# A decoder step on one core: the u projection in whole 128-column blocks, and the Toeplitz rows moved in their queues

## The reference, cut to what matters

```python
z = jnp.einsum('ntd,de->nte', h, w_in)       # columns: q | k | v | u
att = dilated_attn_prompt(q, k, v, rel_bias)  # scores + bias, softmax, values, per head
ssm_y, hT_re, hT_im = s5_branch(u, h0, ...)   # scan over positions, four steps fused by the kernel
x = x + g1 * jnp.einsum('nte,ed->ntd', mixed, w_out)
```

## Time and profile before

| | |
|---|---|
| Time, 3 runs | 965.74, 966.4 (median), 970.36 us |
| Profiled execution | 969.46 us, of which the span from first to last instruction is 967.6 us |
| Mean granted TensorE clock | 0.872 of full speed |
| Busy | PE 789.9 us (82%), DVE 278.7, POOL 166.9, ACT 153.2 |
| Chain that ended last | PE 74%, DVE 8%, DMA 6%, POOL 5% |

### The profile page before, as it was taken

How to read it: one execution, slowest core, us unless ns; L and a number is a source line. 1 busy time by engine, 2 the same in 40 slices (tenths; PEclk the granted TensorE clock), 3 DMA queues, 4 the chain that set the end, 5 groups by cost and what they waited for, 6 DMA issues and landing times.

```text
span 967.6 us, 11960 instructions
## 1 busy us (share of the span) xinstructions
PE 789.9 (82%) x4890; PEld 467.8 (48%) x4890; DVE 278.7 (29%) x693; ACT 153.2 (16%) x324; POOL 166.9 (17%) x258
## 2 busy tenths in 40 slices
PE   2499999999689679676689994499999999999900
PEld 2295688888355355555434554343443444344300
DVE  3633223200012222575313635411111111111028
ACT  1321000000022233313221210000101010000123
POOL 1324100000593000165600000100000000000053
PEclk9878999999655979788899975599999999999955
DMA  9950376700920621709152239667698999999552
GB/s 324 380 181 29 137 223 236 266 4 2 378 107 12 254 83 37 300 3 377 30 162 88 94 126 341 251 238 270 236 397 306 402 401 395 402 399 395 215 196 92
DMA packets 83134, 212.17 MB, mean 219 GB/s; under 512 B 3516, under 2 KB 9948, under 8 KB 80997
## 3 DMA queue, kind: packets, MB, share of 16 engines
q1 hardware_dynamic: 70118, 181.46, 50.9%
q0 software_dynamic: 5472, 19.16, 5.7%
q10 hardware_dynamic: 7488, 10.77, 3.0%
HBM read 197.18 MB, written 17.86 MB: 222 GB/s over the span
## 4 chain that ended last, share of the span: by engine, by line
PE 74%; DVE 8%; DMA 6%; POOL 5%; issue 3%; SPq 3%; ACT 2%; ACTq 0%; POOLq 0%; DVEq 0%
PE ps L2285 17%; PE ps L2288 11%; PE ps L1941 6%; PE ps L1933 6%; PE ps L2195 5%; PE ps L1813 5%; DMA toeplitz<-g_d 3%; PE ps L1902 3%; PE ps L1974 3%; PE ps L1972 3%; PE ps L1992 2%; PE ps L1826 2%; SPq L531 2%; DMA ring<-in_w_out 1%; PE ps L2035 1%
## 5 line engine op out<-in xcount | busy, mean ns | idle before, releaser
L2285 PE MATMUL ps<-ering,xgT 128*128 128x512 f32 x256 | 115.1, 605 | 2.5 <-ACT xgT L801 1.7
L2285 PEld LDWEIGHTS ps<-ering,xgT 128*128 128x128 f32 x256 | 48.6, 194 | 63.4 <-issue 60.1
L2288 PE MATMUL ps<-ering,xgT 128*64 128x512 f32 x320 | 70.7, 595 | 1.2 <-ACT xgT L801 1.2
L1941 PE MATMUL ps<-hT,ring 128*32 128x136 f32 x1024 | 63.1, 424 | 0.0
L1933 PE MATMUL ps<-hT,ring 128*128 128x272 f32 x256 | 59.2, 393 | 0.0
L1941 PEld LDWEIGHTS ps<-hT,ring 128*32 128x32 f32 x1024 | 52.1, 128 | 10.5
L2285 PE MATMUL ps<-ering,aT 128*128 128x512 f32 x128 | 56.2, 593 | 0.0
L768 POOL DMA_INDIRECT xg<-h_d,gidx x13 | 12.3, 949 | 242.8 <-PE ps L1813 210.0
L1933 PEld LDWEIGHTS ps<-hT,ring 128*128 128x128 f32 x256 | 48.5, 190 | 10.3 <-issue 0.4
L1974 PE MATMUL ps<-toeplitz,const 128*128 128x128 f32 (+3 forms) x64 | 32.5, 598 | 25.2 <-DMA toeplitz<-g_d 25.2
L1826 PE MATMUL ps<-ring,silu_c 128*32 128x128 f32 x768 | 27.8, 310 | 24.7 <-DMA ring<-in_ada_w 24.7
(11 more groups left out here) (436 smaller groups left out, 1161.0 us busy)
## 6 DMA issues: line engine op xcount, KB each, us to landing
ering<-in_w_gate SPq DMA_DIRECT2D x16, 2048.0 KB, 17.4
ering<-in_w_up SPq DMA_DIRECT2D x16, 2048.0 KB, 17.4
ering<-in_w_down SPq DMA_DIRECT2D x16, 2048.0 KB, 20.8
ring<-in_ada_w SPq DMA_DIRECT2D x12, 2048.0 KB, 13.1
ring<-in_cache_k SPq DMA_DIRECT2D x8, 1792.0 KB, 10.5
ring<-in_cache_v SPq DMA_DIRECT2D x8, 1792.0 KB, 11.5
ring<-in_w_in SPq DMA_DIRECT2D x4, 2048.0 KB, 22.3
y_d<-ysb ACTq DMA_DIRECT2D x26, 256.0 KB, 6.1
```

The lines of the kernel that those rows point to most:

```text
L1941: ins = mm(out[32 * j:32 * j + 32, N4 * i:N4 * (i + 1)], r[:, c0:c0 + 32], hT[:, k, j::TDEC], start=k == 0, stop=k == KD - 1, tile_positio ...
L2285: return mm(out, lhsT=lhs, rhs=ering[slots[0]][:, cols], start=k == 0, stop=k == n - 1)
L2288: ins = mm(out[c, :], lhsT=lhs[:, c], rhs=ering[slot][:, cols], start=k == 0, stop=k == n - 1, tile_position=(0, HT_ * half))
```

## The change

1. **u in whole blocks.** u is computed as q and k are: 128 by 128 stationary blocks against 272 consecutive tokens. The step interleave is made in the eviction: for each of the four channel groups r of a block and each step j, one copy reads 32 partitions by 68 columns of PSUM with a stride of four columns and writes them to partitions 32 j of u4. So ACT and DVE have 16 copies each for a block, where they had one each.
2. **Toeplitz rows.** SP issues those of heads 0 and 1 before slab 2. Those of heads 2 to 7 leave SP: ACT issues head h's after its last instruction of step 4 (h - 2) + 3. SP then has the slabs alone.

```diff
+    def by_step(z, c, r, j, half):
+        n = HALF // TDEC
+        return (u4[32 * j:32 * j + 32, 4 * c + r, n * half:n * (half + 1)],
+                ps[32 * r:32 * r + 32, 6 * half + z % 2, j:HALF:TDEC])
...
-        for i in (IT_KV + 2, IT_KV + 3):
-            item(i)
-        for h in range(HEADS):
-            if h >= 2:
-                sp.wait_ge(s("S"), QT * (h - 1))
-            sp.dma_start(toep[:, h % 2, :], ...).then_inc(s_toep[h % 2], 16)
-            if h == 3:
-                for i in range(IT_KV + 4, IT_KV + 8):
-                    item(i)
-        for i in range(IT_KV + 8, IT_WO):
+        for h in range(2):
+            sp.dma_start(toep[:, h, :], ...).then_inc(s_toep[h], 16)
+        for i in range(IT_KV + 2, IT_WO):
             item(i)
...
+                for r in range(4):                       # ACT, and DVE with half 1
+                    for j in range(TDEC):
+                        dst, src = by_step(z, c, r, j, 0)
+                        ins = f(dst, src, ACT.Copy)
+                ins.then_inc(s("za"), 1)
...
             f(PTs[:, st % 2, 0:m], ps[:, 2 + st % 2, 0:m], ACT.Copy).then_inc(s("ptr"), 1)
+            if st % QT == QT - 1 and st < QT * (HEADS - 2):
+                h = st // QT + 2
+                act.wait_ge(s("S"), QT * (h - 1))
+                act.dma_start(toep[:, h % 2, :], ...).then_inc(s_toep[h % 2], 16)
...
-                    for k in range(KD if kind != U_ else 0):
+                    for k in range(KD):
                         ins = mm(out, r[:, 512 * k + P * c:512 * k + P * (c + 1)], hT[:, k, cols],
                                  start=k == 0, stop=k == KD - 1)
-                    for i in range(2 if kind == U_ else 0):
-                        for k in range(KD):
-                            c0 = 512 * k + P * c + 32 * (2 * n + i)
-                            for j in range(TDEC):
-                                ins = mm(out[32 * j:32 * j + 32, N4 * i:N4 * (i + 1)], r[:, c0:c0 + 32],
-                                         hT[:, k, j::TDEC], start=k == 0, stop=k == KD - 1, tile_position=(0, 32 * j))
```

More of the change, by code:

```diff
@@ L509, in _ @@
         sp.wait_ge(s("z"), 24)
-        for i in (IT_KV + 2, IT_KV + 3):
-            item(i)
-        for h in range(HEADS):
-            if h >= 2:
-                sp.wait_ge(s("S"), QT * (h - 1))
-            sp.dma_start(toep[:, h % 2, :], bass.AP(g_d.tensor, 640 * h, [[1, P], [1, SEQ]]))\
-                .then_inc(s_toep[h % 2], 16)
-            if h == 3:
-                for i in range(IT_KV + 4, IT_KV + 8):
-                    item(i)
-        for i in range(IT_KV + 8, IT_WO):
+        for h in range(2):
+            sp.dma_start(toep[:, h, :], bass.AP(g_d.tensor, 640 * h, [[1, P], [1, SEQ]])).then_inc(s_toep[h], 16)
+        for i in range(IT_KV + 2, IT_WO):
             item(i)
@@ L872, in _ @@
             kind, c = divmod(z, 4)
-            act.wait_ge(s("z"), 2 * z + 1)
-            dst = qkT[:, 4 * kind + c, 0:HALF] if kind < 2 else u4[:, 4 * c:4 * c + 2, :].rearrange("p a b -> p (a b)")
-            f(dst, ps[:, z % 2, 0:HALF], ACT.Copy, scale=DH ** -0.5 if kind == 0 else 1.0).then_inc(s("za"), 1)
+            if kind < 2:
+                act.wait_ge(s("z"), 2 * z + 1)
+                f(qkT[:, 4 * kind + c, 0:HALF], ps[:, z % 2, 0:HALF], ACT.Copy,
+                  scale=DH ** -0.5 if kind == 0 else 1.0).then_inc(s("za"), 1)
+            else:
+                act.wait_ge(s("z"), 2 * z + 1)
+                for r in range(4):
[3 more added lines that the diff above has]
+                ins.then_inc(s("za"), 1)
             for m in late.get(z, ()):
@@ L910, in _ @@
             f(PTs[:, st % 2, 0:m], ps[:, 2 + st % 2, 0:m], ACT.Copy).then_inc(s("ptr"), 1)
+            if st % QT == QT - 1 and st < QT * (HEADS - 2):
+                h = st // QT + 2
+                act.wait_ge(s("S"), QT * (h - 1))
+                act.dma_start(toep[:, h % 2, :], bass.AP(g_d.tensor, 640 * h, [[1, P], [1, SEQ]]))\
+                    .then_inc(s_toep[h % 2], 16)
             if st == EXP_AT:
@@ L1323, in z_half @@
             dve.wait_ge(s("z"), 2 * z + 2)
-            dst = qkT[:, 4 * kind + c, HALF:NTOK] if kind < 2 else \
-                u4[:, 4 * c + 2:4 * c + 4, :].rearrange("p a b -> p (a b)")
-            ts_(dst, ps[:, 6 + z % 2, 0:HALF], DH ** -0.5 if kind == 0 else 1.0, None, ALU.mult).then_inc(s("zd"), 1)
+            if kind < 2:
+                ts_(qkT[:, 4 * kind + c, HALF:NTOK], ps[:, 6 + z % 2, 0:HALF], DH ** -0.5 if kind == 0 else 1.0, None,
+                    ALU.mult).then_inc(s("zd"), 1)
+                return
+            for r in range(4):
+                for j in range(TDEC):
+                    dst, src = by_step(z, c, r, j, 1)
+                    ins = v.tensor_copy(dst, src)
+            ins.then_inc(s("zd"), 1)
         for j in range(NT):
```

## The result

The changed kernel took 891.1 us in the median of four runs (890.12, 905.84, 888.84, 892.07) against 967.1 of the kernel before on the same chip: a ratio of 0.920, 95% interval 0.917 to 0.923, without the run of 905.84. One number can't be understood without this: the times of the changed kernel lie in two groups some 14 us apart, 888 to 893 and 903 to 906, and the forecast of 905.5 is the upper one. The profiled execution (span 888.3, time 890.12) is of the lower.

What follows compares the result with a forecast made beforehand. The prediction took PE as the bound, busy without a break except for two Toeplitz waits. Terms -33.3, -11.6, -13.6 and -2.4 sum to -60.9, giving 905.5 us from the 966.4 median; range 893 to 919, the forecast's own 900 to 912.

Steps and rivals of the forecast that it cites:

- Part 1: u projection: whole blocks of k's shape take PE from 62.79 to 29.53 us, -33.26; the added copies cost nothing.
- Part 2: Heads 0 and 1's Toeplitz rows issued behind slab 1: PE's wait of 11.63 us goes, -11.6; at worst 0.5 us stays.
- Part 3: Heads 2 to 7's rows issued from ACT: head 4's wait goes, -13.6, and the low clock behind it, -2.4.
- The clock stays up, or rises early: Rival for the attention's first heads: clock held at 1.00 gives 20 us more, 885; rising midway, some 895; 15%.
- the middle case: Within the clock rival: the clock rises midway through the attention's first steps, total some 895 us.
- the rows from ACT: Rival: head 4's rows land no sooner, sharing engines with four slabs; 4.8 of 13.6 us won, 917 us; 11%.
- the copies: Rival in u: at 0.6 us each, 16 copies take 9.6 us a block; u lasts 38.4 us, total 914; 5%.
- ACT's queue: Rival, slower: its six Toeplitz loads each take 22.5 us, like a store beside the slabs, and heads wait; 983 us; 2%.

Runs made afterwards that it cites:

- u alone: Kernel before with only u in whole blocks, Toeplitz rows still in SP's queue as before: 933.15, 933.67, 921.16 and 922.04 us, ratio 0.961.
- Loads alone: Kernel before with only the Toeplitz loads moved in SP's and ACT's queues, u as before: 939.12 and four runs at 923.4 to 927.8 us, ratio 0.958.
- a near copy: Changed kernel with one or three idle DVE additions ahead of the signal that starts the scores: 889.0 to 912.13 us with one, 889.85 to 909.12 with three.
- the kernel before with added work: Kernel before plus 24 full matmuls, results unused, behind the decode bias, in PE's wait for head 0's Toeplitz rows: 960.97 us, ratio 0.994.
- 128 rows: Kernel before with the decode bias multiplying 128 rows instead of 33, the added stationary rows zero: 965.17 us over 12 runs.
- more work behind the bias: Changed kernel plus 8 matmuls of 128 by 128 by 512 columns, results unused, behind the decode bias: 892.13 us, ratio 0.924.
- in step 3: Changed kernel plus 3 matmuls of 128 by 128 by 512 columns, results unused, behind step 3's value product: 893.98 us, ratio 0.925.
- 128 rows in the bias: Changed kernel with the decode bias multiplying 128 rows instead of 33, the added stationary rows zero: 889.67 us, ratio 0.921.
- the two kernels that change more besides: Changed kernel with 128-row bias, heads 0 and 1's rows ahead of all slabs, 2 unused matmuls: 892.33 us; with k and v's stores within u too: 887.0.
- the changed kernel with late rows: Changed kernel with heads 0 and 1's Toeplitz rows issued behind slab 3 again: 900.77, 917.97, 908.69 and 914.55 us, median 911.62.

## Why the prediction was wrong

**Part 1** is right to the last digit: 29.53 us, and the later group of u alone is 33.7 us below before. The copies are hidden, as PE's idle time of 0.0 shows.

**Part 2** is right but for some tenths: PE's wait is 0.81 us, a little over the bound of 0.5, so 10.8 of the 11.6 us went. That the stretch as a whole gave 1.3 us more than forecast is no merit of the sum: the clock fell 5.5 us into the bias and not 3.4, and the bias took 7.32 us where it had taken 9.34.

**Part 3** is right: no wait at head 4, 0.55 at head 5; step 12 to the output won 16.4 us where 13.6 and 2.4 were forecast. Loads alone, in their later run, give 28.0 for parts 2 and 3 together, forecast 27.6.

**The step that failed** is the rival *The clock stays up, or rises early* with its 15%. The mechanism was there; its chance and its price were mis-sized, and with them the low end of the range: 893 took in the middle case as it was priced (895), not as it measures (890). The chance rested on one trace: "two heads of the same steps did not lift it afterwards", and the change "leaves that bias and these steps alone". One execution can't show that. 10 of 23 runs of this code or a near copy were early, and an early return is worth 14.5 us between the two groups of the changed kernel (12 to 18 in the other kernels), not the 10.5 of "895"; in its two traces the way from the first Toeplitz matmul to step 12's scores took 35.9 us early and 50.6 late. The likeliest time of the prediction is a real one: the five runs of the changed kernel with the later return have their median at 904.7.

The rest of the miss, 3.8 us, lies ahead of u: in the profiled run of before the clock fell at 65.4 and was back at 79.0, in that of after 68.0 and 74.9. This goes with the run and not with the change: the kernel before with added work and with 128 rows, the same program up to there, reached u at 174.52 and 174.55 in their traces, and the changed kernel at 174.44.

**What sets the return.** Shown: the fall needs no idle PE (33-row bias), and comes with an idle PE just as well (128 rows). In the changed kernel the share of early returns goes with what PE does between u and head 1: 10 of 23 as it is or nearly so, 12 of 12 with more work behind the bias or in step 3, and with 128 rows in the bias 6 of 6, or 18 of 19 with the two kernels that change more besides. In the kernel before, 128 rows alone make 3 of 12; that its wait of 11.6 us holds against them is argued, not shown.

An early return is not undone by head 4's wait: u alone, which keeps it, is 12 us faster in its early runs. In the kernel before with added work most of the gain was lost behind that wait, where the clock stayed down for 44 us instead of 17. Nor are the parts worth more together than apart. In the late runs u alone gives 33.7 us and the loads alone 28.0 (one run), in all 61.7, and both together 62.4.

Open: what tells an early run from a late one of the same code; and why the kernel before is so rarely early, 5 of 67. Its wait ahead of head 0 is not the whole answer, for u alone has it too (2 of 4 early), as has the changed kernel with late rows (1 of 4 at 901); and the loads alone, with the old u, are early in 4 of 5. Each half of the change raised the share, and runs as few as these set no share for either.

The other rivals: the rows from ACT did land sooner; the copies bound nothing; ACT's queue did not starve PE, though not for the reason given. Its six loads were issued in 0.33 to 0.35 us each, so none held ACT for the time it took to land; the danger on that queue was the store of 4.43 us ahead of head 0, which the forecast did not look at, and which became 10 us of waiting as soon as the bias no longer covered it.

## What to carry to other kernels

A stall that is removed can be worth more than its length, or less: look at the granted clock on both sides of it, and give the other level of the clock a real chance wherever a stretch of short or thin matmuls stands next to it, since one trace shows one of two outcomes. Price the parts of a change in runs of one kind: here late runs add up (33.7 and 28.0 against 62.4 together), while the medians, which mix early and late runs in other shares, would give 39.5 and 40.8 apart and 63.3 together. And before an operation is moved, ask which issue on another engine's queue it covers.

## What was not expected of the hardware

- The same program ran its first heads at 1.2 or at 2.4 GHz, 888 to 893 or 903 to 906 us, on one chip in one sitting; the return came within 0.6 us of head 1's first scores in seven of the nine traces of early runs (in the other two within added matmuls), and in step 10 in all eight of late ones.
- A matmul of 33 rows against one of 128, same columns and count: the clock fell within the bias in 14 of 14 traces with 33 rows, PE being busy without a break in 13 of them, and in none of four with 128. The bias took 7.32 us with the fall in it, and 6.50 without.
- The third output store on ScalarE's queue was held at issue for 4.43 to 13.40 us, from kernel to kernel, while slabs of SP's were on their way; within u the three stores took 0.44, 2.42 and 0.60 us.
- Copies of 32 partitions by every fourth of 272 PSUM columns cost 218 (ACT) and 225 ns (DVE): no price for the stride.
